# Small expert jobs on unsplit fp32 weights, two 64-column stationary blocks at a time

## What is computed

```python
def swiglu(x, w_gate, w_up, w_down):
    return (jax.nn.silu(x @ w_gate) * (x @ w_up)) @ w_down

def moe_swiglu(x, w_router, w_gate, w_up, w_down):
    logits = (x @ w_router).astype(jnp.float32)
    top_vals, top_idx = lax.top_k(logits, TOP_K)
    top_w = jax.nn.softmax(top_vals, axis=-1)
    gates = jnp.sum(jax.nn.one_hot(top_idx, N_EXPERTS, dtype=jnp.float32) * top_w[..., None], axis=-2)
    out = jnp.zeros_like(x)
    for e in range(N_EXPERTS):
        out = out + gates[..., e:e + 1].astype(x.dtype) * swiglu(x, w_gate[e], w_up[e], w_down[e])
    return out
```

## Time and profile before

| | us |
|---|---|
| median of three runs | 1384.07 |
| span of the profiled execution | 1383.7 |
| TensorE busy | 1331.8 (96%) |
| DVE busy | 1147.2 (83%) |
| ACT busy | 990.3 (72%) |
| mean granted TensorE clock | 0.995 of full |
| HBM read / written | 438.04 MB / 8.54 MB |

### The profile page before, as it was taken

How to read it: one execution, slowest core, us unless ns; L and a number is a source line. 1 busy time by engine, 2 the same in 40 slices (tenths; PEclk the granted TensorE clock), 3 DMA queues, 4 the chain that set the end, 5 groups by cost and what they waited for, 6 DMA issues and landing times.

```text
span 1383.7 us, 19518 instructions
## 1 busy us (share of the span) xinstructions
PE 1331.8 (96%) x6863; PEld 1145.6 (83%) x6863; DVE 1147.2 (83%) x1052; ACT 990.3 (72%) x959; POOL 132.9 (10%) x119
## 2 busy tenths in 40 slices
PE   9999999999999999999999999999999999999987
PEld 8988888888997888878879888878888887787865
DVE  5776545467665899999999999999999999899986
ACT  5545444446455787888878878887888888787884
POOL 2000000000000088910010000000000002000000
PEclk9999999999999999999999999999999999999999
DMA  9655656567542799999999999999999999999980
GB/s 323 240 159 194 189 194 195 183 211 220 185 141 98 264 403 411 408 408 411 397 403 413 409 411 412 402 411 401 407 412 410 400 413 407 411 408 401 373 362 31
DMA packets 135590, 447.36 MB, mean 323 GB/s; under 512 B 8409, under 2 KB 30053, under 8 KB 123246
## 3 DMA queue, kind: packets, MB, share of 16 engines
q1 hardware_dynamic: 130560, 430.99, 81.3%
q0 software_dynamic: 3072, 8.91, 1.9%
q10 hardware_dynamic: 1902, 6.71, 1.4%
HBM read 438.04 MB, written 8.54 MB: 323 GB/s over the span
## 4 chain that ended last, share of the span: by engine, by line
PE 54%; DMA 18%; DVE 15%; issue 8%; ACT 4%; SPq 1%; ACTq 0%; DVEq 0%
PE banks L1249 16%; PE banks L1798 14%; DVE w_lo L2021 11%; DMA raw<-in_o_exp_gate 9%; PE banks L1283 6%; DMA raw<-in_o_exp_down 5%; PE banks L1557 4%; PE banks L1871 4%; PE banks L1819 4%; ACT w_hi L704 3%; DMA raw<-in_o_exp_up 2%; DMA raw<-in_e_w_in 1%; PE banks L1782 1%; SPq L402 1%; PE banks L1835 1%
## 5 line engine op out<-in xcount | busy, mean ns | idle before, releaser
L2021 DVE TENSOR_TENSOR w_lo<-raw,w_hi 128x1792 fp32r<-128x1792 f32 (+1 forms) x454 | 919.2, 2064 | 119.4 <-PE banks L1249 49.8
L704 ACT ACTIVATE w_hi<-raw 128x1792 fp32r<-128x1792 f32 (+1 forms) x454 | 784.6, 1737 | 270.9 <-PE banks L1249 79.7
L1819 PE MATMUL banks<-w_lo,x_hi 128*128 128x448 f32 x512 | 131.0, 378 | 16.3 <-DVE w_lo L2021 15.8
L1798 PE MATMUL banks<-w_hi,x_hi 128*128 128x448 f32 x512 | 128.0, 372 | 0.0
L1819 PEld LDWEIGHTS banks<-w_lo,x_hi 128*128 128x128 f32 x512 | 91.4, 188 | 42.0 <-DVE w_lo L2021 35.9
L1819 PE MATMUL banks<-w_hi,x_hi 128*128 128x448 f32 x512 | 125.7, 368 | 0.3 <-ACT w_hi L704 0.2
L1798 PE MATMUL banks<-w_lo,x_hi 128*128 128x448 f32 x512 | 125.7, 367 | 0.1
L1798 PE MATMUL banks<-w_hi,x_lo 128*128 128x448 f32 x512 | 125.3, 366 | 0.0
L1249 PE MATMUL banks<-w_hi,x_lo 128*128 128x512 f32 (+1 forms) x304 | 108.6, 357 | 0.3 <-DVE x_lo L2056 0.3
L1819 PEld LDWEIGHTS banks<-w_hi,x_hi 128*128 128x128 f32 x512 | 96.4, 189 | 14.3 <-ACT w_hi L704 1.4
L1249 PE MATMUL banks<-w_hi,x_hi 128*128 128x512 f32 (+1 forms) x304 | 108.1, 356 | 0.0
(11 more groups left out here) (343 smaller groups left out, 1863.6 us busy)
## 6 DMA issues: line engine op xcount, KB each, us to landing
raw<-in_o_exp_gate SPq DMA_DIRECT2D x128, 896.0 KB, 8.0
raw<-in_o_exp_up SPq DMA_DIRECT2D x128, 896.0 KB, 9.1
raw<-in_o_exp_down SPq DMA_DIRECT2D x96, 1024.0 KB, 8.5
raw<-in_o_exp_down SPq DMA_DIRECT2D x32, 512.0 KB, 7.7
raw<-in_o_w_qkv SPq DMA_DIRECT2D x12, 1024.0 KB, 5.8
raw<-in_e_ffn_gate SPq DMA_DIRECT2D x11, 1024.0 KB, 5.3
raw<-in_e_ffn_up SPq DMA_DIRECT2D x11, 1024.0 KB, 5.2
raw<-in_e_ffn_down SPq DMA_DIRECT2D x11, 1024.0 KB, 5.0
```

The lines of the kernel that those rows point to most:

```text
L704: act.activation(w_hi[:, at % HI, 0:size], raw[:, at % RAW, 0:size], ACT.Copy).then_inc(hi_made, 1)
L1798: mm = pe.matmul(bank[first + f][:, 0:CUT // 2], x[:, 2 * k + kk, 0:P], w[:, kk, f * (CUT // 2):(f + 1) * (CUT // 2)], start=start and kk ...
L1819: mm = pe.matmul(bank[first + f][:, 0:CUT // 2], x_two[:, 2 * k + kk, :], w[:, kk, f * (CUT // 2):(f + 1) * (CUT // 2)], start=start and k ...
L2021: ve.tensor_tensor(w_lo[:, at % LO, 0:size], raw[:, at % RAW, 0:size], w_hi[:, at % HI, 0:size], ALU.subtract)\
```

## The change

Small jobs no longer use split weights or split activations. `x_small` (64 columns, fp32) replaces `x_two`, `hid_rows` (fp32) replaces `hid_two`. `small_up` and `small_down` multiply them straight with the fp32 tile in `raw`, and each product is given a `tile_position`: the even chunk of the contraction goes to columns 0 to 63 of the array and to rows 0 to 63 of the bank, the odd chunk to columns 64 to 127 and rows 64 to 127. The two halves are added afterwards, as before. Only the 12 tiles of wide jobs are split (`WIDE_AT`), with slots of `w_hi` and `w_lo` counted over wide tiles alone (`wide_no`). A slot of `raw` that held a wide tile is free on `lo_made`, one that held a small tile on `tile_used`, that is, when TensorE is through with it (`slot_free`). The steps `high_small`, `low_small` and DVE's `gathered_small` go away.

```diff
+WIDE_AT = (0, 1, 2, 3, 4, 6, 8, 9, 16, 18, 20, 22)
-        x_two = x_hi[:, :, P:2 * P]
+        x_small = scores.rearrange("p b n -> p (b n)")[:, CUT:CUT + KC * SMALL].rearrange("p (k t) -> p k t", k=KC)
-        hid_two = m_hi[:, 4:8].rearrange("p a (b s) -> p (a b) s", s=P)[:, 0:PARTS]
+        hid_rows = hid_s.rearrange("p (c t) -> p c t", c=PARTS)
...
+            def slot_free(i, j, b, final):
...
+                if was in tiles:
+                    sp.wait_ge(lo_made, wide_no(tiles.index(was), j, b) + 1)
+                else:
+                    sp.wait_ge(tile_used, tile_at(was, j, b) + 1)
...
             def small_up(first, k, i, j, b):
 
-                hi, lo = up_tiles(i)
-
-                def product(w, start=False, stop=False):
+                w = raw_tile(i, UP, CUT)
+                pe.wait_ge(*landed(i, j, b))
+                for f in range(2):
                     for kk in range(2):
-                        for f in range(2):
-                            mm = pe.matmul(bank[first + f][:, 0:CUT // 2], x_two[:, 2 * k + kk, :], w[:, kk, f * (CUT // 2):(f + 1) * (CUT // 2)],
-                                           start=start and kk == 0, stop=stop and kk == 1, skip_group_check=True)
-                    return mm
-
-                wait_high(tile_at(i, j, b))
-                product(hi, start=k == 0)
-                wait_tile(tile_at(i, j, b))
-                product(lo, stop=k == 3).then_inc(tile_used, 1)
+                        mm = pe.matmul(bank[first + f][kk * SMALL:(kk + 1) * SMALL, 0:CUT // 2], x_small[:, 2 * k + kk, :],
+                                       w[:, kk, f * (CUT // 2):(f + 1) * (CUT // 2)], start=k == 0, stop=k == 3,
+                                       tile_position=(0, kk * SMALL), skip_group_check=True)
+                mm.then_inc(tile_used, 1)
...
             def small_down(k, i, j, b, stop=False, last=False):
...
+                def product(half, kk, at):
+                    return pe.matmul(bank[4 + half][at * SMALL:(at + 1) * SMALL, :], hid_rows[:, 2 * k + kk, :],
+                                     w[:, kk, half * HALF:(half + 1) * HALF], start=False, stop=stop and k == 3,
+                                     tile_position=(0, at * SMALL), skip_group_check=True)
...
                 for half in range(2):
-                    product(half, 0)
-                wait_tile(tile_at(i, j, b))
-                product(0, 1, end=stop and k == 3)
-                product(1, 1, end=stop and k == 3).then_inc(tile_used, 1)
+                    if k < 3:
+                        product(half, 0, 0)
+                        mm = product(half, 1, 1)
+                    else:
+                        mm = product(half, 0, half)
```

More of the change, by code:

```diff
@@ L339, in tile_at, with wide_tiles, wide_no, wide_size @@
             return n if b is None else n + STEP_TILES * b
[L341 to L350, removed]
+        def wide_tiles(j=None, final=False):
+            return OPEN_WIDE if j is None else FINAL_WIDE if final else WIDE_AT
+        def wide_no(w, j=None, b=None):
+            n = MOE_T + w
+            if j is not None:
+                n = n + STEP_WIDE * BLOCKS * j
+            return n if b is None else n + STEP_WIDE * b
+        def wide_size(w):
+            return UP if w < 8 else TILE if w < 11 else TILE // 2
+        def landed(i, j=None, b=None):
+            r = (MOE_T - SKIP + i) // RAW
+            if j is not None:
+                r = r + (DUO_TILES // RAW) * j
+            if b is not None:
+                r = r + (STEP_TILES // RAW) * b
+            return tile_loaded[(MOE_T - SKIP + i) % RAW], 16 * r + 16
         def chunk_of(q):
@@ L525, in _ @@
             for k in range(4):
-                down(small, BLOCKS - 1, k, k, last, BLOCKS)
-            nj = last + 1
+                down(small, BLOCKS - 1, k, STEP_TILES + k, last, BLOCKS - 1, True)
             for i in range(4):
-                load(DUO_TILES * nj + (GATE1_T + i), rows_of(o_ple_gate[0], i), slot=(GATE1_T + i) % RAW)
+                load_part(rows_of(o_ple_gate[0], i), STEP_TILES + 4 + i, last, BLOCKS - 1, True)
             for b in range(4):
@@ L1168, in block @@
                 high_up(j, b)
[L1169 to L1172, removed]
+                st(2, 5, j, b)
+                used(3, j, b)
                 silu_wide(j, b)
@@ L1225, in _ @@
             block(3, last, final=True)
[L1226 to L1231 removed]
+            nj = last + 1
+            for i in range(3):
+                used(i, last, BLOCKS)
+                split(None, GATE1_T + i, (GATE1_T + i) // RAW + (DUO_TILES // RAW) * nj)
             for half in range(2):
@@ L2607, in _, with gate_low @@
             block(3, last, adding=2, final=True)
-            for i in range(STEP_TILES, STEP_TILES + 3):
-                lo(i, last, BLOCKS - 1, True)
             nj = last + 1
+            def gate_low(i):
+                ve.wait_ge(hi_made, wide_no(i, nj) + 1)
+                ve.tensor_tensor(w_lo[:, (GATE1_T + i) % LO], raw[:, (GATE1_T + i) % RAW], w_hi[:, (GATE1_T + i) % HI], ALU.subtract)\
+                    .then_inc(lo_made, 1)
+            ve.wait_ge(tile_used, tile_at(FINAL_WIDE[-1], last, BLOCKS - 1) + 1)
+            for i in range(LO):
+                gate_low(i)
             scattered()
             lows(5)
-            split(GATE1_T + LO - 1 + DUO_TILES * nj, GATE1_T + LO - 1)
-            split(GATE1_T + LO + DUO_TILES * nj, GATE1_T + LO)
+            ve.wait_ge(tile_used, GATE1_T + DUO_TILES * nj + 1)
+            gate_low(LO)
             rsqrt(5)
```

254 lines of the change are left out of this document (112 added, 142 removed).

## The result

| kernel | median, us | runs | profiled span, us |
|---|---|---|---|
| before | 1383.13 (1381.40 to 1384.07) | 4 | 1383.7 |
| changed | 1413.34 (1411.16 to 1415.47) | 4 | 1409.4 |

The changed kernel is slower by a ratio of 1.0216, 95% interval 1.0200 to 1.0232, about 30 us. The forecast was 1411. The number was right by luck: the mechanism behind it did not occur, as this part shows.

What follows compares the result with a forecast made beforehand. The DMA queue bounds the kernel before (55.3 us a block); after, TensorE was to, with the small job at 24.0 us against 22.1: 1.9 over 15 blocks, +28, less 1 at the end, gives 1411 us, range 1381 to 1495.

Steps and rivals of the forecast that it cites:

- What bounds the kernel: In the experts, before the change: DMA queue needs 55.3 us a block, TensorE 52.6, leaving TensorE 2.7 us of room.
- Splits removed: Half of ACT's and DVE's splits go, with 31.0 us of TensorE waits; worth zero while DMA is the bound.
- Pairs: Small job's half products, each sharing its time with one of the other 64 columns: 18.0 us a block, best case.
- Stagger: In each run of small products one half product stands alone at an end: eight runs, 3.1 us a block.
- Switches: Changes between full-array and half-column products: 16 a block at 0.18 us, 2.9 us a block.
- Sum: Small job takes 18.0 + 3.1 + 2.9 = 24.0 us against 22.1 that fit; TensorE the bound by 1.9 a block.
- Slots: Small tiles' slots freed on TensorE's use: zero, up to 1 us a block; as rival, starved queue, 1399 us, chance 0.02.
- The end: Last block's small down no longer waits for the hidden values' split: -1 us, bounds -2.5 and +1.
- What would show it: Signs in the experts: DMA share about 0.97, GB/s about 393, DVE and ACT halved, single small tile about 2.2 us.
- no overlap at all: Rival: column-block products never run side by side; small job 36.0 us, up to 38.9 with switches; 1593 to 1636, chance 0.15.
- DMA stays the bound: Rival: small job stays under 22.1 us, so transfers set the time, 1381.5 to 1387 us; chance 0.28.
- Weight loads are not hidden: Rival: 64-column weight loads wait for running products, about 0.06 each, 5.5 us more a block; 1494 us, chance 0.10.

Runs made afterwards that it cites:

- The run with the copies: Changed kernel's small products with the slots of before, multiplying from a copy ACT puts in the ring of high halves: 1377.80 us, 0.9968 of the kernel before.
- the run with half columns: Changed kernel with 224 instead of 448 columns in the small jobs' gate and up products: 1403.58 us, 1.0159 of the kernel before.

## Why the prediction was right in number and wrong in its step

The forecast came from a TensorE that would be the bound by 1.9 us a block (+28 us, chance 0.45). That did not happen. The loss came from the slot rule, which stood in the sum with zero and among the rivals with 2 in 100 and 1399 us. That an excess that is not there and a loss that was left out are both near 28 us is luck.

*What bounds the kernel*: right. The DMA queue; less TensorE work brought nothing, and the room of 2.7 us measured as about 3.5.

*Splits removed, zero*: right while the transfers bind. The run with the copies spares DVE's half of these splits, while ACT still makes a copy of each tile; it is 0.3% faster, and how much of that is due to the splits is not shown.

*Pairs, 18.0 us*: right. 0.376 and 0.43 per pair, and without pairs the time came within 4 us of what their doubling gives.

*Stagger, 3.1 us*: wrong; it is zero. This term made the excess: 18.0 + 2.9 = 20.9 us fits into 22.1. I had taken the array as one line of work in which a product may only overlap the one ahead. The two column blocks start together, whatever the order in the code.

*Switches, 2.9 us*: right in size. Around small tile 7 of the changed kernel:

```profile
802.46 0.98 PE L1819 MATMUL banks<-w_lo,x_hi 128*128 128x448 f32 x4
803.37 1.94 PE L1887 MATMUL banks<-raw,work 128*64 128x512 f32 x8
805.24 1.08 PE L1819 MATMUL banks<-w_hi,x_hi 128*128 128x448 f32 x4
806.15 0.97 PE L1819 MATMUL banks<-w_hi,x_lo 128*128 128x448 f32 x4
```

The group at 802.46 has its 0.81 until 803.27, the small tile starts 0.10 later; four pairs are 1.72, which leaves 0.15 to the next group's start, and that group takes 0.91 instead of 0.81. Together 0.35, against 0.15 + 0.2 by the transposes. The Trainium skill (TensorEngine Tiling, Key Properties) says that a change of tiling mode drains TensorE; the trace agrees, and gives 0.35 us for the way in and out.

*Sum*: wrong. Corrected by the runs, TensorE needs 52.6 - 19.4 + 20.9 = 54.1 us a block of the queue's 55.3, and by the sum alone the time would not have moved. The run with changed products and old slots shows just that.

*Slots, "zero, up to 1 us a block"*: this is the step that failed. It is 1.8 us a block in the changed kernel, and 2.1 (32 over 15) as the only change. The bound was sought by asking whether TensorE keeps up over a block, and held against an allowance of some 5 us from landing to use. The kernel before has already 4.7 to 6.7 us there at the small tiles in the profile's issue and landing records, which I did not read tile by tile. With the rule it is 7 to 9 at five tiles. And a lag within a block is enough: with a queue that is the bound throughout, no later stretch gives the lost us back.

*The end, -1 us*: right in sign, and smaller. From the start of the last wide down product to the end the two kernels need 49.1 and 48.7 us (from 1360.67). The wait before small down is gone; from the start of the first scatter products it is 44.1 and 44.8 us.

*What would show it*: GB/s near 393 and half the splits were seen, but a DMA share of 0.97 and a busy TensorE were not. The mean share fell only to 1.01, and TensorE stayed at 95%. Those two signs told the wrong bound from the right one. A single gate or up tile takes 1.75 us between its wide neighbours (829.39 to 831.14 in the single records), not 2.2: the stagger is missing.

*Rivals*: "no overlap at all" is refuted by the pairs. "DMA stays the bound" named the right bound, but not the time, which it put at 1387 at most. "Weight loads are not hidden" did not come, and its price was misread: the loads of the earlier trace rows have 64 rows and 128 columns, not 64 columns. The Trainium skill (TensorE: Matmul & The Clock Gate, The mechanism) has loads overlap running matmuls only for another row group; the trace does not agree for column blocks. Within a run, PEld's rows show loads of 64 columns, pairs of 0.14 us, at 810.73, 811.10 and 811.48 under products that keep their distance of 0.376:

```profile
810.73 0.14 PEld L1839 LDWEIGHTS banks<-raw,scores 128*64 128x64 f32 x2 [0.23 <-issue]
811.10 0.14 PEld L1839 LDWEIGHTS banks<-raw,scores 128*64 128x64 f32 x2 [0.23 <-issue]
811.48 0.14 PEld L1839 LDWEIGHTS banks<-raw,scores 128*64 128x64 f32 x2 [0.23 <-issue]
```

## What to carry to other kernels

When a change moves the release of a buffer from one engine to another, take from the trace, buffer by buffer, the time from landing to release before, and set beside it when the new engine comes to that buffer; a mean over a loop hides it. If the transfer queue is the bound, each us in which it is short is lost for good, and making the engines faster brings back only what it frees sooner (here 10 of 31 us, for 6.0 us less TensorE work in each of 16 blocks); releasing the buffer earlier, even by a copy that looks like wasted work, does. Take the faster product and keep the old release.

## What the runs showed of the hardware

- Two fp32 products in column blocks 0 to 63 and 64 to 127 of the array start 6 to 7 ns apart (13 in the other order) and run at full rate (a pair each 0.376 us at 448 columns, 0.43 at 512). It does not matter whether they are issued by turns or two and two: 1413.3 and 1413.9 us.
- Idle time of TensorE can cost clock. In the run with half columns, TensorE stood for 3.48 us from 813.8 to 817.3, and the next stretches have a granted clock of 0.75 and 0.91 (whole run 0.967):

```profile
815.00:820.00 5.00, 2.72 (x7) 2.15 (x8) 2.29 (x1) 1.91 (x1) 0.00 (x0) 0.75 1.03 418
820.00:825.00 5.00, 5.00 (x25) 3.53 (x24) 2.29 (x1) 2.91 (x3) 0.00 (x0) 0.91 1.02 412
```

The group of four 512-column products at 817.28 takes 1.93 us instead of 1.2, which fits the lower of the clock's two levels, 1.2 GHz instead of 2.4. So work left out of TensorE is partly given back. The changed kernel itself shows it once, in its last block, where the granted clock is 0.50 from 1345 to 1350 us and the group that waited 3.72 us takes 2.07:

```profile
1345.67 2.07 PE L1852 MATMUL banks<-w_hi,m_hi 128*128 128x512 f32 x4 [3.72 <-ACT w_hi L1096]
```

The prediction took the clock to stay at 1.0; in the blocks before, it does but for 3.4 us at 963 and at 1191.
- The mean DMA share is a weak sign. It stood at 1.01 with 385.6 GB/s on the weight queue and at 1.02 with 398.3; the GB/s in stretches of 4 us showed the holes at once.
